# The up products of two expert loops: x's high and low parts as one product of 480 columns, their sums joined by VectorE

## What is computed

```python
s1 = einsum(q[:, :, 0], sk1); s2 = einsum(q[:, :, 1], sk2)   # 8 heads, 128 keys each
... top 16 of each, top 16 of the 256 sums -> expert, gate = softmax(top_s)
u = u_tab[expert]; v = v_tab[expert]
act = gelu(einsum('cd,chkd->chk', xc, u))
return einsum('chk,chkd->cd', gate * act, v)
```

## Time and profile before

| | |
|---|---|
| three runs | 2905.26 us median, 2894.94 to 2908.54 |
| the profiled execution | 2900.71 us, span 2898.9 us, granted clock 0.978 |
| busy, share of the span | PE 96%, PEld 91%, DVE 71%, ACT 53%, POOL 23% |
| matmuls | 21855 |
| the fused loops | about 542 to 1065 us and 1594 to 2113 us from the span's start |

### The profile page before, as it was taken

The page is one execution under the profiler, slowest core; times in us unless marked ns, Lnnn a source line. Parts: engine busy times, 40 slices in busy tenths (PEclk is TensorE's granted clock), DMA queues, the critical chain, the costliest instruction groups (busy, mean ns, idle before and its releaser), DMA issues.

```text
span 2898.9 us, 61371 instructions
## 1 busy us (share of the span) xinstructions
PE 2768.7 (96%) x21855; PEld 2638.6 (91%) x21855; DVE 2064.1 (71%) x4489; ACT 1538.8 (53%) x3323; POOL 657.0 (23%) x708
## 2 busy tenths in 40 slices
PE   8898989999999999999889999999998999999999
PEld 8688988999999987898889999999997899986999
DVE  5748886787777865769877777777676756555565
ACT  7453344555555544652445555555555655555554
POOL 3622571021111113213660010000044410112100
PEclk9999999999999999999999999999998999998999
DMA  4034416687877853146336777676643046451464
GB/s 152 30 111 154 143 51 203 217 295 248 268 242 261 271 168 117 59 148 186 101 96 223 228 240 237 225 246 217 192 146 121 28 150 194 153 167 37 146 184 135
DMA packets 151348, 492.07 MB, mean 170 GB/s; under 512 B 17776, under 2 KB 35632, under 8 KB 151184
## 3 DMA queue, kind: packets, MB, share of 16 engines
q1 hardware_dynamic: 135120, 435.70, 46.7%
q0 software_dynamic: 15488, 54.25, 6.6%
q10 hardware_dynamic: 576, 0.03, 0.0%
HBM read 480.77 MB, written 9.14 MB: 169 GB/s over the span
## 4 chain that ended last, share of the span: by engine, by line
PE 87%; DVE 5%; ACT 4%; POOL 2%; issue 1%; DMA 0%; DVEq 0%; POOLq 0%; ACTq 0%; SPq 0%
PE banks L825 64%; PE banks L1010 7%; PE banks L1031 3%; PE banks L1141 2%; POOL x_lo L2536 2%; PE banks L861 2%; PE banks L925 2%; PE banks L856 1%; ACT w_hi L525 1%; ACT arena L1498 1%; PE banks L1243 1%; PE banks L1274 1%; DVE arena L2097 0%; PE banks L1237 0%; DVE w_lo L532 0%
## 5 line engine op out<-in xcount | busy, mean ns | idle before, releaser
L532 DVE TENSOR_TENSOR w_lo<-ring,w_hi 128x512 fp32r<-128x512 f32 x1464 | 1021.3, 705 | 585.0 <-ACT w_hi L525 555.8
L525 ACT ACTIVATE w_hi<-ring 128x512 fp32r<-128x512 f32 x1464 | 914.7, 631 | 823.2 <-PE banks L825 776.9
L825 PE MATMUL banks<-gated_all,w_hi 128*128 128x240 f32 (+1 forms) x5120 | 892.6, 277 | 10.5 <-DVE gated_all L2184 10.5
L825 PE MATMUL banks<-x_hi,w_hi 128*128 128x240 f32 (+2 forms) x3072 | 868.8, 283 | 25.4 <-POOL x_lo L2536 9.0
L825 PE MATMUL banks<-x_hi,w_lo 128*128 128x240 f32 (+2 forms) x3072 | 857.1, 279 | 0.0
L825 PE MATMUL banks<-x_lo,w_hi 128*128 128x240 f32 (+2 forms) x3072 | 856.0, 279 | 0.0
L825 PEld LDWEIGHTS banks<-gated_all,w_hi 128*128 128x128 f32 x5120 | 777.8, 190 | 17.2 <-issue 9.3
L825 PE MATMUL banks<-gated_all,w_lo 128*128 128x240 f32 (+1 forms) x2560 | 709.6, 277 | 0.0
L825 PEld LDWEIGHTS banks<-x_hi,w_hi 128*128 128x128 f32 x3072 | 583.3, 190 | 45.5 <-POOL x_lo L2536 18.3
L825 PEld LDWEIGHTS banks<-x_hi,w_lo 128*128 128x128 f32 x3072 | 582.0, 189 | 0.0
L825 PEld LDWEIGHTS banks<-x_lo,w_hi 128*128 128x128 f32 x3072 | 581.4, 189 | 0.6
(11 more groups left out here) (336 smaller groups left out, 2981.8 us busy)
## 6 DMA issues: line engine op xcount, KB each, us to landing
ring<-in_peer_v SPq DMA_DIRECT2D x256, 512.0 KB, 3.6
ring<-in_peer_u SPq DMA_DIRECT2D x192, 512.0 KB, 4.5
arena<-in_peer_u SPq DMA_DIRECT2D x64, 512.0 KB, 3.7
ring<-in_mlp_up SPq DMA_DIRECT2D x64, 512.0 KB, 3.6
ring<-in_mlp_down SPq DMA_DIRECT2D x64, 512.0 KB, 3.6
ring<-w_peer_query SPq DMA_DIRECT2D x32, 512.0 KB, 3.6
ring<-w_fox_proj SPq DMA_DIRECT2D x24, 512.0 KB, 4.2
ring<-w_nsa_proj SPq DMA_DIRECT2D x20, 512.0 KB, 3.6
```

The lines of the kernel that those rows point to most:

```text
L525: act.activation(w_hi[:, hn % SPLITS], raw_half(hn), ACT.Copy).then_inc(hi_ready, 1)
L532: dve.tensor_tensor(w_lo[:, hn % SPLITS], raw_half(hn), w_hi[:, hn % SPLITS].bitcast(F32), ALU.subtract)\
L825: mm = pe.matmul(out, w_at(w), x, start=start and j == 0, stop=stop and j == 2, skip_group_check=True)
```

## The change

In the two peer stages (`early` not 0), `up` is no longer made by `project`. `x_hi` and `x_lo` become halves of one tensor `x_both`, and for each of the 8 feature chunks PE issues one product of `w_hi` with both (2 x 240 columns, into columns 0 to 239 and 240 to 479 of the bank) and one of `w_lo` with `x_hi` into the first 240. DVE then adds the two halves of the bank with a `reduce_sum` into a new buffer `up_out` and raises `halves_joined`; ACT's Gelu waits for that and reads `up_out`. PE's `up` waits for `halves_joined` in place of `act_ready` before it writes a bank again. On DVE, the `split_lo` of the first half of chunk n+3 moves from between `gate` and `gated_rest` to behind the `reduce_sum`, ahead of `gate`. Buffers in `work` are laid out anew (256 columns each).

```diff
-        x_hi = placed("x_hi", [P, NC, X_STEP], (MOVED_AT - 4 * META) % ROW, F32R)[:, :, 0:T0]
-        x_lo = placed("x_lo", [P, NC, X_STEP], (MOVED_AT - 4 * META) % ROW, F32R)[:, :, 0:T0]
+        x_both = placed("x_both", [P, 2, NC, X_STEP], (MOVED_AT - 4 * META) % ROW, F32R)
+        x_hi, x_lo = x_both[:, 0][:, :, 0:T0], x_both[:, 1][:, :, 0:T0]
...
-        act_out = work[:, 0:2 * T0].rearrange("p (a t) -> p a t", a=2)
-        act_gated = work[:, 2 * T0:3 * T0]
+        act_out = work[:, 0:2 * SEQ].rearrange("p (a t) -> p a t", a=2)
+        act_gated, up_out = work[:, 2 * SEQ:3 * SEQ], work[:, 3 * SEQ:4 * SEQ]
...
                 def up(b, n, freed, i=None):
 
                     if freed is not None:
-                        pe.wait_ge(act_ready, plus(freed, i, 4))
-                    project(n, 6 + b, tokens, i, x_run=s["x0"] - 1 if freed is None and not early else None)
+                        pe.wait_ge(halves_joined if early else act_ready, plus(s["g0"] - a0 + freed if early else freed, i, 4))
+                    if not early:
+                        project(n, 6 + b, tokens, i, x_run=s["x0"] - 1 if freed is None else None)
+                        return
+                    out = banks[:, 6 + b, 0:2 * tokens]
+                    for half in range(2):
+                        pe.wait_ge(lo_ready, plus(2 * n + half + 1, i, 16))
+                        for c4 in range(4):
+                            c, own = 4 * half + c4, slice(c4 * P, (c4 + 1) * P)
+                            pe.matmul(out.rearrange("p (j t) -> p j t", j=2), w_hi[:, half_of(n, half), own],
+                                      x_both[:, :, c, META:META + tokens], start=c == 0, stop=False, skip_group_check=True)
+                            mm = pe.matmul(out[:, 0:tokens], w_lo[:, half_of(n, half), own], x_hi[:, c, META:META + tokens],
+                                           start=False, stop=c == NC - 1, skip_group_check=True)
+                        mm.then_inc(half_used, 1)
...
                         follow(split_hi, act, n, i)
-                    act.wait_ge(half_used, plus(2 * n + 2, i, 16))
+                    if early:
+                        act.wait_ge(halves_joined, plus(s["g0"] + k + 1, i, 4))
+                    else:
+                        act.wait_ge(half_used, plus(2 * n + 2, i, 16))
                     if freed is not None:
                         act.wait_ge(gated_f32_ready, plus(freed, i, 4))
-                    act.activation(act_out[:, b, 0:tokens], banks[:, 6 + b, 0:tokens], func).then_inc(act_ready, 1)
+                    src = up_out[:, 0:tokens] if early else banks[:, 6 + b, 0:tokens]
+                    act.activation(act_out[:, b, 0:tokens], src, func).then_inc(act_ready, 1)
...
                     if n > n0 or i is not None:
                         follow(split_lo, dve, n, i)
+                    if early:
+                        dve.wait_ge(half_used, plus(2 * n + 2, i, 16))
+                        out = banks[:, 6 + b, 0:2 * tokens]
+                        dve.reduce_sum(up_out[:, 0:tokens], out.rearrange("p (j t) -> p t j", j=2), AX_X).then_inc(halves_joined, 1)
+                        if n > n0 or i is not None:
+                            split_lo(dve, 2 * (n + 1) + SPLITS, i)
                     dve.wait_ge(act_ready, plus(a0 + k + 1, i, 4))
                     if k >= 1 or early:
                         dve.wait_ge(gated_ready, plus(d0 + k, i, 4))
                     gate(b, plus(early + k, i, 4))
-                    if n > n0 or i is not None:
+                    if (n > n0 or i is not None) and not early:
                         split_lo(dve, 2 * (n + 1) + SPLITS, i)
```

More of the change, by code:

```diff
@@ L148, in lay_out_stages @@
     bank_frees = rope_chunks = dense_steps = fused_steps = peer_tiles = gate_groups = early = picks = 0
-    pairs = pair_chunks = 0
+    pairs = pair_chunks = joined = 0
     bars = squares_n = sums = presums = finals = pool_finals = kept = x_runs = 0
     for at, (kind, q) in enumerate(STAGES):
-        s = dict(q, kind=kind, at=at, n0=n, k=seen.get(kind, 0), bf0=bank_frees, r0=rope_chunks, d0=dense_steps, a0=fused_steps, e0=early,
+        s = dict(q, kind=kind, at=at, n0=n, k=seen.get(kind, 0), bf0=bank_frees, r0=rope_chunks, d0=dense_steps, a0=fused_steps, g0=joined, e0=early,
                  pt0=peer_tiles, gg0=gate_groups, pk0=picks, bar=bars, sq0=squares_n, su0=sums, ps0=presums, hf0=finals, hp0=pool_finals,
@@ L168, in lay_out_stages @@
             dense_steps += q["n"]
+            joined += q["n"] - q["early"] if q["early"] else 0
             fused_steps += q["n"] - q["early"]
@@ L463, in build_program @@
         compared, hit_ready = sem("compared"), sem("hit_ready")
-        act_ready, gated_ready = sem("act_ready"), sem("gated_ready")
+        act_ready, gated_ready, halves_joined = sem("act_ready"), sem("gated_ready"), sem("halves_joined")
         scores_ready, max_ready, exp_done, turned, turned_stored, av_done, mixed = (sem(n) for n in (
```

## The result

The changed kernel takes 3072.19 us (median of 6 runs, 3070.34 to 3075.85), the kernel before 2901.78 us (6 runs, 2893.18 to 2908.54): a ratio of 1.0587, 95% interval 1.0567 to 1.0606. It is slower by 170 us, where 3067 us had been forecast. The profiled execution took 3071.21 us with a span of 3069.4 us and a mean granted clock of 0.979.

The account below looks back on a forecast made before the run. PE was taken to bound the kernel before, the round of DVE and ACT after the change; 24, 30, 55 and 58 us make 167 us, added to 2900.7 us to give 3067 us, range 3000 to 3118 us.

Parts of the forecast that it names:

- The round of DVE and ACT: Both fused loops: hand-overs in program order make a plain step 5.69 us, against PE's 5.3 to 5.4 us.
- Its two waits: DVE idle 1.0 us behind the reduction for Gelu and ACT's high split, and 0.47 us behind gate for the high part.
- Gathered steps: Steps with a dot or addition on DVE: 48 dots add 1.14 us each, 48 additions 1.20 us each.
- The reduction: DVE's 192 new sums of 480 PSUM elements to 240: 0.65 us each, bounds 0.40 and 0.81 us.
- The sum: Both loops: 24 and 30 us for longer steps, 55 us for dots, 58 us for additions, together 167 us.
- PE's part: 1536 wide products in both loops: 0.0105 us less each, 16 us, vanishing in PE's waits.
- The 512-column row: Trace row of products starting every 0.229 us, scaled by 480 / 512 to 0.215 us for a wide product.
- The clock: Rival: PE idling in gathered steps drops the clock to 1.2 GHz, 264 us more, 3331 us in all; chance 4%.
- The load rival: DVE's and ACT's load decides, not their order: PE stays the bound, 2885 us, at the limit 2862 us; chance 5%.
- LDWEIGHTS as the measure: Rival in PE's loops: weight loads busy 99%, so removing 8 of 48 should pay; gain ends at 39 us.
- PE's waits: PE waits for the low part that releases down in nearly every step, about 180 us in all.

Follow-up runs that it names:

- e1: Changed kernel with the low split of n+3's first half back between gate and gated_rest, the join kept: 2918.79 us, ratio 1.0050.
- e6: Changed kernel with the 96 dots and additions for gathered tokens moved from the end of DVE's step to right behind the reduction: 2963.10 us, ratio 1.0220.
- e7: Changed kernel with ACT's high split of n+3's first half moved ahead of Gelu, DVE untouched: 2920.93 us, ratio 1.0055.
- e3: Changed kernel with the 96 dots and additions for gathered tokens cut from 1024 columns to 16: 2972.92 us, ratio 1.0243.
- e5: Kernel before with the wide products alone: no join, low split in its old place, sum of the low part left out: 2889.07 us, ratio 0.9949.
- e2: Changed kernel without the join: Gelu reads the bank, sum of the low part left out, low split stays ahead of gate: 2894.30 us, ratio 0.9977.
- e4: Changed kernel with each product of 480 columns made as two of 240: 3077.44 us, ratio 1.0595.
- e8: Changed kernel with the low split back behind gate and the 96 dots and additions right behind the reduction: 2901.03 us, ratio 0.9987.
- e9: Changed kernel with low split back behind gate, dots and additions right behind the reduction, and products of 240 columns: 2901.65 us, ratio 1.0005.

## Why the prediction was right, and what was off

- **The round of DVE and ACT** was walked through as 5.69 us; it is 5.62 to 5.73 us. Its two waits, given as 1.0 and 0.47 us, are 0.99 and 0.47. e1, e6 and e7 change nothing but the place of instructions, take 109 to 153 us off, and so show that the order is what binds and not the amount of work.
- **Gathered steps**: 1.14 and 1.20 us more each, so 6.83 and 6.89 us; measured 6.77 to 6.94 us. The three first additions were priced like the others (1.20 us) and cost some 0.8 us each, so the sum is about 1 us too high by them. e3 (99 us less with the instructions small) and e6 (109 us less with them in the gap) show it from two sides.
- **The reduction**, taken as 0.65 us by the slope of two rows with few outputs, took 650 ns. 240 outputs of two elements each cost nothing beyond that slope here.
- **The sum** of the loops, 167 us, measured 164. One term was set a little wrong: the first loop did not run at 5.44 us a step throughout before. By Gelu's starts it was 5.32 to 5.38 us for its first 42 regular steps and 5.44 us for the later ones. The stretch that I read lay in the second part. That the forecast lies within 5 us of the measured time is in part luck: the loops cost 3 us less than the sum, 6 us came from outside them, for which the sum has no term, and runs of the kernel before scatter by 15 us.
- **PE's part** was mis-sized: 0.0105 us saved per wide product were 5 ns in most steps. An up product of a chunk takes 2.65 us against 2.69 us, so 0.04 / 8; against the 2.72 us of the first loop's second half it is 9 ns. `down` gives some of it back (see the end), so that both loops are 7.6 us shorter in e5 than before, where 16 us had been taken. The 512-column row was not the nearest to a product whose columns come in two runs of 240, or the loss is elsewhere; no run tells these apart. In e2's timeline of PE, wide and narrow products in turn:

```profile
900.89 0.39 PE L1065 MATMUL banks<-x_both,w_hi 128*128 128x480 f32 x1
901.12 0.28 PE L1067 MATMUL banks<-x_both,w_lo 128*128 128x240 f32 x1
901.23 0.38 PE L1065 MATMUL banks<-x_both,w_hi 128*128 128x480 f32 x1
...
902.88 0.38 PE L1065 MATMUL banks<-x_both,w_hi 128*128 128x480 f32 x1
```

  Six pairs in 1.99 us are 0.332 us a pair. This term did not count in the forecast, since it was hidden (e4), but it bounds what the change can bring in this kernel: 8 us by the steps, 14 us by e5's median, 0.3% to 0.7% by its interval.
- **The clock** did not fall: 1.00 in both loops, with PE idle for some 1.5 us in each gathered step. The rival of 3331 us is refuted.
- **The load rival** (DVE has room, so nothing is lost) was right about the room, and wrong about what it means in this order. It came true in e8, where the order lets the room be used.
- **LDWEIGHTS as the measure** (the Trainium skill, Perfetto Trace Analysis, "Identifying the Most-Contended Engine"). The Trainium skill takes the busy share of the weight loads as a sign of how near TensorE is to its limit. The trace of the kernel before agrees, where it is 99% and PE is the bound. What the prediction made of it, that fewer loads should then pay, came out only in part. In e5 a sixth of the loads is gone, their share is 95%, and PE is still the bound:

```profile
545.00:1050.00 505.00, 505.00 (x3779) 481.65 (x3778) 406.57 (x662) 292.05 (x564) 71.85 (x63) 1.00 0.79 260
```

  The loops gained 8 us of 1026. The time went nearly with the columns: 720 of them took 0.332 us as two products, and 3 x 0.112 = 0.336 us as three.
- **PE's waits** were given as about 180 us under the low part. The view of waits has 133.8 us for PE behind L2201, since the modelled end of a product lies behind the start of the next; by starts the loops are 164 us longer and lose another 8 us of PE work, so by this sum PE stood for some 172 us more than before.

## What to carry to other kernels

Where two engines pass work back and forth in program order, write one trip around with its waits and compare it with the step of the bounding engine; busy shares of 74% and 45% hid a round that set the step here. A new instruction in such a round is paid not only by its length but by whatever it puts between a producer and its consumer: move the other engine's order along (e7), or put independent work into the gap (e6, e8). And before a product is made wider, read what the pace of the wide form is in the trace: a third fewer products in `up` were worth 1.5% of its time in most steps.

## What was not expected

- With narrow products the first loop's pace changes in its middle, behind the gathered tokens' sum: 2.69 us for a chunk's 24 products, then 2.72 us, in the kernel before and in e9. With wide products it does not (2.65 us for `up` and 2.70 us for `down` on average in both parts). More than half of what the wide products gain lies in this second part. The cause is open.
- `down` itself, which is unchanged, takes 2.69 to 2.72 us beside wide products, 2.70 us on average, where it took 2.69 us beside narrow ones, so over a third of a small gain goes back.
- `gate` took 574 ns in the changed kernel's first loop, 600 ns before, and the high split 615 ns against 633 ns: both a few per cent shorter. PE's idle time does not explain it for `gate`: in e2, where PE hardly stands, `gate` took 585 ns, and in e1, where PE stands in the gathered steps, 605 ns. In the changed kernel no ACT instruction runs beside `gate`, as ACT waits 1.25 us for it; no run tests whether that is the reason.
